# q and k normalised and transposed between the chunks of the last v block

## The reference

```python
def _nat_mixer(h, w_qkv, q_norm, k_norm, rpb, w_o):
    qkv = (h @ w_qkv).reshape(bsz, seq, 3, N_HEADS, HEAD_DIM)     # 1024 -> 3 * 1024
    q = _rmsnorm(qkv[:, :, 0], q_norm)                            # per head of 64
    k = _rmsnorm(qkv[:, :, 1], k_norm)
    v = qkv[:, :, 2]
    ...
    s = jnp.einsum('bhjqrc,...', q_blk, k_band) * scale + bias    # 16 heads, bands of 32 columns
    prob = jax.nn.softmax(...)
    o = jnp.einsum('bhjqrc,brjchd->bjqhd', prob, v_band)
    return out @ w_o
```

## Time and profile before

| | |
|---|---|
| median of three runs | 825.47 us (824.51 to 826.08) |
| the profiled execution | 826.0 us, span 824.2 us |
| PE busy | 746.4 us, 91% of the span |
| DVE, ACT, POOL busy | 375.5, 234.1, 186.5 us |
| DMA | 243.95 MB, mean 296 GB/s |

### The profile page before, as it was taken

How to read it: one execution, slowest core, us unless ns; L and a number is a source line. 1 busy time by engine, 2 the same in 40 slices (tenths; PEclk the granted TensorE clock), 3 DMA queues, 4 the chain that set the end, 5 groups by cost and what they waited for, 6 DMA issues and landing times.

```text
span 824.2 us, 10762 instructions
## 1 busy us (share of the span) xinstructions
PE 746.4 (91%) x4121; PEld 413.8 (50%) x4121; DVE 375.5 (46%) x668; ACT 234.1 (28%) x424; POOL 186.5 (23%) x206
## 2 busy tenths in 40 slices
PE   2977879899999998899999967998999999989997
PEld 2746735633443433345878856466343443433465
DVE  6999452632322222226667858134422233222264
ACT  5551113511101111015575537143001101110163
POOL 7776210320110101000457260030210111100000
PEclk9997979999999999999999979998999999999999
DMA  7062071999999999998589570770999999999851
GB/s 206 27 138 103 9 305 34 424 408 416 422 421 421 420 422 421 419 415 315 195 219 298 189 283 1 306 295 12 330 423 423 419 421 421 421 421 416 332 219 51
DMA packets 66452, 243.95 MB, mean 296 GB/s; under 512 B 21441, under 2 KB 22481, under 8 KB 44641
## 3 DMA queue, kind: packets, MB, share of 16 engines
q1 hardware_dynamic: 62208, 239.71, 73.8%
q0 software_dynamic: 1408, 3.24, 1.8%
q10 hardware_dynamic: 2784, 0.30, 0.3%
HBM read 240.55 MB, written 1.64 MB: 294 GB/s over the span
## 4 chain that ended last, share of the span: by engine, by line
PE 66%; DVE 11%; DMA 7%; SPq 7%; POOL 4%; issue 3%; ACT 3%; ACTq 0%; DVEq 0%
PE PS L1837 21%; PE PS L1581 11%; PE PS L1867 10%; DMA ring<-in_moe_w_up 7%; PE PS L1877 5%; PE PS L2057 3%; PE PS L1765 3%; SPq L472 3%; SPq L473 2%; PE PS L1707 2%; PE PS L1806 2%; SPq L490 2%; PE PS L1961 2%; PE PS L1722 1%; POOL qrs L729 1%
## 5 line engine op out<-in xcount | busy, mean ns | idle before, releaser
L1837 PE MATMUL PS<-ring,xe 128*64 128x512 f32 x1024 | 226.2, 593 | 13.6 <-DMA ring<-in_moe_w_up 11.3
L1837 PEld LDWEIGHTS PS<-ring,xe 128*64 128x64 f32 x1024 | 77.2, 137 | 157.6 <-issue 157.5
L1867 PE MATMUL PS<-ring,actT 128*64 128x512 f32 x512 | 116.9, 598 | 1.7 <-DVE actT L1345 1.4
L644 POOL COPY xe<-xg 128x512 f32 x60 | 47.7, 794 | 296.8 <-PE PS L1837 265.0
L1359 DVE TENSOR_TENSOR olo<-PS,ohi 128x512 fp32r<-128x512 f32 x64 | 44.3, 692 | 123.1 <-ACT ohi L912 123.1
L1345 DVE COPY actT<-PS 128x256 f32<-128x256 f32 x32 | 13.6, 425 | 167.3 <-PE PS L1848 167.3
L912 ACT ACTIVATE ohi<-PS 128x512 fp32r<-128x512 f32 x64 | 38.3, 598 | 152.9 <-PE PS L1867 152.9
L1066 DVE SCALAR_TENSOR_TENSOR ringr<-ring,gT,dwh 128x512 fp32r<-128x512 f32 x80 | 63.1, 841 | 26.4 <-ACT dwh L775 25.1
L904 ACT ACTIVATE act<-PS 128x256 f32<-128x256 f32 x32 | 12.3, 384 | 218.1 <-PE PS L1837 218.1
L1867 PEld LDWEIGHTS PS<-ring,actT 128*64 128x64 f32 x512 | 34.7, 136 | 67.0 <-issue 67.0
L1581 PE MATMUL PS<-ringr,rawh 128*128 128x512 f32 x160 | 63.3, 396 | 0.8 <-DVE ringr L1066 0.8
(11 more groups left out here) (320 smaller groups left out, 978.0 us busy)
## 6 DMA issues: line engine op xcount, KB each, us to landing
ring<-in_moe_w_down SPq DMA_DIRECT2D x64, 1024.0 KB, 20.1
ring<-in_moe_w_gate SPq DMA_DIRECT2D x52, 1024.0 KB
ring<-in_moe_w_up SPq DMA_DIRECT2D x52, 1024.0 KB
ring<-in_moe_w_gate SPq DMA_DIRECT2D x24, 512.0 KB
ring<-in_moe_w_up SPq DMA_DIRECT2D x24, 512.0 KB
ring<-in_nat_w_qkv SPq DMA_DIRECT2D x6, 2048.0 KB
ring<-in_ple_w_gate SPq DMA_DIRECT2D x4, 2048.0 KB
ring<-in_s_w_out SPq DMA_DIRECT2D x2, 2048.0 KB
```

The lines of the kernel that those rows point to most:

```text
L644: pool.tensor_copy(xe[:, e % 4, :, :], xg[:, :, bass.ds(first, CAP)]).then_inc(S("xe_ready"), 1)
L1837: ins = mm(PS[CAP * h_:CAP * h_ + CAP, 0, :].rearrange("p (u f) -> p u f", u=2), xe[:, (2 * p + h_) % 4, k, :], wv[h_][:, k], start=k == 0 ...
L1867: ins = mm(PS[CAP * h_:CAP * h_ + CAP, 2 + n, :], actT[:, k, CAP * h_:CAP * h_ + CAP], wd[h_][:, k, 512 * n:512 * n + 512], start=k == 0, ...
```

## The change

Squares, sums and the power of q and k are done while block 5 (the second of v) is split and multiplied, and PE transposes tile 0 between chunks 1 and 2 of it and tile 1 between chunks 2 and 3. `sq` holds both tiles. Blocks 4 and 5 are evicted later on DVE (block 4 behind the multiplies), block 5 behind `qT` and `kT` on both engines. `qT` and `kT` move from slot 4's memory to the last 8 KB of ring slots 1 and 2, `vb` to the last 8 KB of slot 0. POOL copies v in two parts of 512 columns, four DMAs each, after block 4 and after block 5; `values(0)` waits for the first part, `values(4)` for the second. SP fills slot 4 once the transposes and block 5 are done; the down part of slot 0 waits until the value products are done.

```diff
         qk = at("qk", [P, TT, 2 * NH, HD], F32, A_HI)
         vt = at("vt", [P, TT, D], F32, A_HI + 16384)
-        sq = at("sq", [P, 2 * NH, HD], F32, A_XG)
+        sq = at("sq", [P, TT, 2 * NH, HD], F32, A_XG)
         qss = at("qss", [P, TT, 2 * NH], F32, A_W)
         qms = at("qms", [P, TT, 2 * NH], F32, A_W + 256)
         qrs = at("qrs", [P, TT, 2 * NH], F32, A_W + 512)
         qkw = at("qkw", [P, 2], F32, A_W + 1024)
-        qT = at("qT", [P, NH // 2, T], F32, A_XG + 16384)
-        kT = at("kT", [P, NH // 2, T], F32, A_XG + 24576)
+        qT = at("qT", [P, NH // 2, T], F32, A_R + 1 * RS * 4 + 16384)
+        kT = at("kT", [P, NH // 2, T], F32, A_R + 2 * RS * 4 + 16384)
         oT = at("oT", [P, NH // 2, T], F32, A_O)
         bias = at("bias", [P, NPR, NB_, P], F32, A_H)
         maskb = at("maskb", [P, NB_, BC, ROWS], F32, A_S)
-        vb = at("vb", [P, 2, D], F32, A_HI + 24576)
+        vb = at("vb", [P, 2, D], F32, A_R + 16384)
         V_OF = ((vt, 0), (vb, 0), (vb, 1), (vt, 1))
         prob = at("prob", [P, 4, NB_, P], F32, A_XG)
         probT = at("probT", [P, 2, NB_, P], F32, A_XG + 8192)
...
                         if i == 0:
                             sp.wait_ge(S("x_ready"), 1)
                         else:
-                            sp.wait_ge(S("pv_done"), NPR)
+                            sp.wait_ge(S("k_T"), 2 * TT)
+                            sp.wait_ge(S("split_done"), 4 * dense.index(IT["qkv"][5]) + 4)
+                    if i == 1 and items[m0 + e][0] == 5:
+                        sp.wait_ge(S("pv_done"), NPR)
+                        load_down(m0 + 1, True)
                     load_gate_up(m0 + e)
-                    load_down(m0 + e, True)
+                    if i == 0 or e != 1:
+                        load_down(m0 + e, True)
                 for p in range(3, NP + 1):
                     if p < NP:
                         load_pair(m0 + 2 * p)
...
                 pool.tensor_tensor(qrs[:, t, :], qms[:, t, :], mhalf[:, :], ALU.pow)\
                     .then_inc(S("qrs_ready"), 1)
-            pool.wait_ge(S("qkv_a"), 6)
-            pool.wait_ge(S("qkv_d"), 6)
-            for n, (p0, p1, t, src0) in enumerate(((0, 96, 0, 32), (96, P, 1, 0), (0, 32, 0, 96), (32, P, 1, 0))):
-                pool.dma_start(vb[p0:p1, n // 2, :], vt[src0:src0 + p1 - p0, t, :]).then_inc(S("v_moved"), 16)
+            for c in range(2):
+                pool.wait_ge(S("qkv_a"), 5 + c)
+                pool.wait_ge(S("qkv_d"), 5 + c)
+                cs = slice(512 * c, 512 * c + 512)
+                for n, (p0, p1, t, src0) in enumerate(((0, 96, 0, 32), (96, P, 1, 0), (0, 32, 0, 96), (32, P, 1, 0))):
+                    pool.dma_start(vb[p0:p1, n // 2, cs], vt[src0:src0 + p1 - p0, t, cs]).then_inc(S("v_moved_later" if c else "v_moved"), 16)
             moe(1)
             norm_pow(5)
...
                     ac.dma_start(qkw[64 * d:64 * d + 64, c:c + 1], I[nm][0].rearrange("(p a) -> p a", a=1))\
                         .then_inc(S("qkw_loaded"), 16)
             load_router(ac, 1)
-            for w in range(7):
-                if 0 < w < 6:
-                    dense_hi(IT["qkv"][w], 0, 4)
-                if w:
-                    v_ = w - 1
-                    ac.wait_ge(S("split_done"), 4 * dense.index(IT["qkv"][v_]) + 4)
-                    dst = qk[:, 0, 8 * v_:8 * v_ + 8, :].rearrange("p a d -> p (a d)") if v_ < 4 else \
-                        vt[:, 0, 512 * (v_ - 4):512 * (v_ - 4) + 512]
-                    ac.wait_ge(S("rstd_ready"), NI[3] + 1)
-                    ac.activation(dst, PS[:, 2 * (v_ % 2), :], ACT.Copy, scale=rstd[:, 0:1]).then_inc(S("qkv_a"), 1)
-                if w == 5:
-
+            def qkv_evict(v_):
+                ac.wait_ge(S("split_done"), 4 * dense.index(IT["qkv"][v_]) + 4)
+                dst = qk[:, 0, 8 * v_:8 * v_ + 8, :].rearrange("p a d -> p (a d)") if v_ < 4 else \
+                    vt[:, 0, 512 * (v_ - 4):512 * (v_ - 4) + 512]
+                ac.wait_ge(S("rstd_ready"), NI[3] + 1)
+                ac.activation(dst, PS[:, 2 * (v_ % 2), :], ACT.Copy, scale=rstd[:, 0:1]).then_inc(S("qkv_a"), 1)
+            for w in range(1, 6):
+                dense_hi(IT["qkv"][w], 0, 4)
+                qkv_evict(w - 1)
+                if w == 4:
+
+                    ac.wait_ge(S("qkv_d"), 4)
+                    ac.wait_ge(S("qkv_a"), 4)
                     for t in range(TT):
-                        ac.wait_ge(S("qkv_d"), 4)
-                        ac.wait_ge(S("qkv_a"), 4)
-                        if t:
-                            ac.wait_ge(S("qss_ready"), t)
-                        ac.activation(sq[:, :, :], qk[:, t], ACT.Square).then_inc(S("sq_ready"), 1)
+                        ac.activation(sq[:, t], qk[:, t], ACT.Square).then_inc(S("sq_ready"), 1)
             ac.wait_ge(S("qkw_loaded"), 64)
             link(ac.activation(qkw8[:, :], qkw[:, 0:1], ACT.Copy, scale=1 / math.sqrt(HD)))
...
                     ac.activation(qT[:, 4 * n:4 * n + 4, P * t:P * t + P],
                                   PS[:, 4 + n, :].rearrange("p (a t) -> p a t", a=4), ACT.Copy,
                                   scale=qkw8[:, 0:1]).then_inc(S("qT_ready"), 1)
+            qkv_evict(5)
             for a in range(NPR + 2):
                 if a < NPR:
...
                 ve.wait_ge(S("rstd_ready"), NI[3] + 1)
                 ts(dst, PS[:, n % 4, :], rstd[:, 1:2], None, ALU.mult).then_inc(S("qkv_d"), 1)
-            for w in range(6):
-                if w:
-                    dense_lo(IT["qkv"][w], 0, 4)
-                if w:
-                    qkv_evict(w - 1)
+            for w in range(1, 5):
+                dense_lo(IT["qkv"][w], 0, 4)
+                qkv_evict(w - 1)
             for t in range(TT):
                 ve.wait_ge(S("sq_ready"), t + 1)
-                ve.tensor_reduce(qss[:, t, :], sq[:, :, :], AX.X, ALU.add).then_inc(S("qss_ready"), 1)
+                ve.tensor_reduce(qss[:, t, :], sq[:, t], AX.X, ALU.add).then_inc(S("qss_ready"), 1)
                 ve.wait_ge(S("qss_ready"), t + 1)
                 ts(qms[:, t, :], qss[:, t, :], 1.0 / HD, EPS, ALU.mult, ALU.add).then_inc(S("qms_ready"), 1)
-            qkv_evict(5)
+            dense_lo(IT["qkv"][5], 0, 4)
             for t in range(TT):
                 ve.wait_ge(S("qrs_ready"), t + 1)
                 tt(qk[:, t], qk[:, t], bc(qrs[:, t, :], 2, HD), ALU.mult).then_inc(S("qkn_ready"), 1)
+            qkv_evict(4)
             ve.wait_ge(S("qkw_loaded"), 64)
             for t in range(TT):
                 for n in range(2):
                     ve.wait_ge(S("k_T"), 2 * t + n + 1)
                     ts(kT[:, 4 * n:4 * n + 4, P * t:P * t + P], PS[:, 6 + n, :].rearrange("p (a t) -> p a t", a=4),
                        qkw[:, 1:2], None, ALU.mult).then_inc(S("kT_ready"), 1)
+            qkv_evict(5)
             def scores(a):
                 b = a % 4
...
             dense_mm(IT["qkv"][0], 0, 0, 1)
             raw_T(1, 1)
             dense_mm(IT["qkv"][0], 0, 1, 4)
-            for w in range(1, 6):
-                if w >= 2:
-                    pe.wait_ge(S("qkv_a"), w - 1)
-                    pe.wait_ge(S("qkv_d"), w - 1)
-                dense_mm(IT["qkv"][w], 2 * (w % 2), 0, 4)
-            for t in range(TT):
+            def qk_T(t):
+
                 pe.wait_ge(S("qkn_ready"), t + 1)
                 for b, what in ((4, "q_T"), (6, "k_T")):
                     for n in range(2):
...
                             ins = pe.transpose(PS[:, b + n, P * a:P * a + P],
                                                qk[:, t, hd:hd + 2, :].rearrange("p a d -> p (a d)"), ident[:, :])
                         ins.then_inc(S(what), 1)
+
+            for w in range(1, 6):
+                if w >= 2:
+                    pe.wait_ge(S("qkv_a"), w - 1)
+                    pe.wait_ge(S("qkv_d"), w - 1)
+                if w < 5:
+                    dense_mm(IT["qkv"][w], 2 * (w % 2), 0, 4)
+            dense_mm(IT["qkv"][5], 2, 0, 2)
+            qk_T(0)
+            dense_mm(IT["qkv"][5], 2, 2, 3)
+            qk_T(1)
+            dense_mm(IT["qkv"][5], 2, 3, 4)
             pe.wait_ge(S("qT_ready"), 4)
             pe.wait_ge(S("kT_ready"), 4)
-            pe.wait_ge(S("qkv_a"), 6)
-            pe.wait_ge(S("qkv_d"), 6)
+            pe.wait_ge(S("qkv_a"), 5)
+            pe.wait_ge(S("qkv_d"), 5)
             def scores(a):
...
             def prob_T(a):
                 pe.wait_ge(S("prob_ready"), a + 1)
+                if a == 0:
+                    pe.wait_ge(S("qkv_a"), 6)
+                    pe.wait_ge(S("qkv_d"), 6)
                 if a >= 2:
                     pe.wait_ge(S("probT_ready"), a - 1)
                 for j in range(NB_):
...
             def values(a):
-                if a == 0:
-                    pe.wait_ge(S("v_moved"), 64)
+                if a % 4 == 0:
+                    pe.wait_ge(S("v_moved_later" if a else "v_moved"), 64)
```

## The result

The changed kernel took 821.88 us as the median of six runs (817.8 to 825.58), the kernel before 825.91 beside it: a ratio of 0.9934, 95% interval 0.991 to 0.9958. Measured again, beside the kernel before once more, it took 819.06 beside 827.64, ratio 0.9894 (0.9867 to 0.992). The kernel got faster, by 0.7% in one measurement and 1.1% in the other. The forecast, 817.6 on 825.47, is a ratio of 0.9905: between the two and inside the second interval only. The first median lies 0.6 us above the upper end of the range; carried over to the 825.47 that the range was made for, its ratio gives 820.0.

The account below looks back on a forecast made before the run. Bound: a compute chain up to pair 0, then a DMA-bound tail that shifts with it. Order of the stretch -7.0 and faster first scores -0.85 gave 825.47 - 7.85 = 817.6 us; range 815.2 to 821.3 (0.85).

Parts of the forecast that it names:

- The bound and the one-to-one shift: Compute chain up to pair 0: each microsecond saved in attention moves the DMA-bound tail equally, about 7.9 us; not-reaching-the-end rival 0.04.
- the 7.9 that I had named: First refill after pair 0 and everything behind it: predicted to come about 7.9 us earlier.
- The stretch: Block 4's end to the first scores: 17.15 us instead of 24.17, so -7.0.
- the first stall: TensorE idle before block 5's first chunk, waiting for VectorE's low part: 1.85 us; rival that both stalls vanish, 0.05.
- The second stall: TensorE idle before the first transposes, waiting for the first multiply: 0.9 us.
- The 0.85: First scores at full clock: VectorE uses them 1.2 us after their start instead of 2.08, saving 0.85 more.
- The rule against the row: VectorE's low parts under POOL's power: no slowing assumed; rival by the skill's contention rule, with clock loss, 828.3 us, chance 0.04.
- The clock: Rival: TensorE's clock falls to 0.50 in the new stalls, losing 3.0 us, 0.9 of it possibly hidden; chance 0.13.
- the 24.17 of attention: First use of a score to the product with w_o: the eight pairs were to follow one another as before.
- The v copies: Second part wanted by the fifth value product: in time at 495, cost 0; rival late, up to +2.2 us, chance 0.04.
- The bound, all of SP's 5 MB in front: Second v copies waiting for all 5 MB, 12.5 us, plus 6.4: landing at 507.8, 2.2 us late.
- The range: Measured time of the whole changed kernel: 815.2 to 821.3 us, given 0.85.

Follow-up runs that it names:

- moves_only: The kernel before with only the moves in memory, slot 4's earlier prefill and the v copies in two parts, old order kept; ratio to before 0.9996.
- before_again: The kernel before, unaltered, traced a second time; one execution, no ratio; 25.35 us from block 4's end to VectorE's first use of a score.
- late_prefill: The changed kernel with slot 4 filled only after the last value product, as before; ratio to the kernel before 0.992.

## Why the prediction was right, point by point

*The bound and the one-to-one shift*: right, although the 6.77 is not the 7.9 that I had named, by what layer 0 and the stage behind attention did in these two traces. The first refill and the end moved alike (6.77 and 6.8), and moves_only shows that an earlier prefill alone is worth nothing.

*The stretch*: forecast 17.2 from block 4's end to the scores, measured 17.14; the first stall 1.85 against 1.87; 16 transposes 1.75 against 1.72. The second stall was 0.40 and not 0.9, since chunks 0 and 1 ended later than I had put them and the multiply came 0.3 sooner, each counted from block 4's end. Forecast to the first use 7.85 less, measured 7.95. The 0.85 in it for faster first scores was read from one trace and is partly luck: in before_again those scores were at full clock already, and the gain to the first use is 7.1 to 7.2 against it.

*The rule against the row*: right to follow the row. The low parts under the power take 0.67 each. The rule of the Trainium skill, GPSIMD Engine Reference, Key points, holds for the bias adds and says nothing of how much GpSimd must read before it matters; the power's 32 elements a partition slowed nothing here.

*The clock*: the rival was real and cheap, one trace of six at 1.2 us, where I had reckoned 2.1 to 3.0. What I left out is what the scores at full clock lead to: a wait of 2.45 us in place of 1.21, behind which the clock fell in five of eight traces and took 0.2 to 1.8 back. I had carried the 24.17 of attention over as it was. That it came out to the hundredth in the changed kernel's first trace is luck, for the two traces got there differently: slow scores and a short wait before, full clock and a long wait after.

*The v copies*: the step was right in outcome and its size was off. I took 5.6 us to landing for the second part, from a row in which the 3 MB in front had been issued six microseconds before and were nearly through; it measured up to 10.0, so to 501.1, and what hid it is that the fifth value product comes only at 507.92. The bound, all of SP's 5 MB in front, came to 18.9 after issue (12.5 + 6.4) and was further off still: the truth lies between, since the last of SP's 5 MB landed six microseconds after the copies. With the copies whole, which are 1 MB in place of half, it was 14.5. The Trainium skill, DMA: Bandwidth & Descriptors, Queues, rings and completion order, has two statements on this: a DMA engine takes turns between its queues packet by packet, and a completion is a strongly ordered write that lands only after every earlier write of that DMA engine, whichever its queue. The copies passing part of a queue agree with the first; no run here can show what the second adds.

*The range*: too narrow at the top for one measurement of six runs. The stretch is worth 7.2 to 8.0 by the traces, where the first measurement's ratio is worth 5.4 of 825.47 and the second's 8.7. That the difference is the clock elsewhere is likely but not shown: from the product with w_o to the first refill it took 57.87 us at a clock of 0.94 before, 56.67 at 0.97 in the changed kernel and 55.07 at 1.00 when it was measured again, and in front of the stage, with the same code, block 4's end moves by up to 5.8 us between traces.

## What to carry to other kernels

A serial chain of small steps between two products is best started ahead of the part of the first that doesn't feed it (here v's block): it hides the chain, and it takes away the waits behind which the clock fell. Where exactly its last steps stand between the chunks matters little (7.5 against 0.5 us here). When a change moves a load forward in one queue, look at the small transfers issued behind it on another, and price them between two bounds, their time on idle engines and their time with all of the load in front; here they came out between the two every time, and the same reorder with the copies in one part was slower than the kernel before. And after removing a wait, follow the next bound: here POOL's power, then VectorE's order, then TensorE's clock.

## What the runs showed of the hardware that was not expected

SBUF-to-SBUF copies of 512 columns (four, half a megabyte) landed 2.1 to 2.5 us after issue on idle DMA engines, 7.4 to 8.1 behind 2 MB (late_prefill) and 7.4 to 10.2 behind 5 MB (six traces). The first of these, in the changed kernel:

```profile
DMA to landing us min/median/max: 2.1/2.3/2.5
```

Copies of 1024 columns took 5.4 to 6.4 in the kernel before, 8.7 to 10.6 behind 2 MB and 9.8 to 14.5 behind 5 MB, and still landed 3.7 us ahead of the last of these 5. The granted clock can fall after a wait of 1.9 us that follows unbroken matmuls, and mostly doesn't: the same code kept 1.00 in five traces and was at 0.50 in one. Behind the wait of 2.45 us in attention it fell in nine of twelve traces, at a cost of 0.2 to 1.8 us where nothing else held TensorE up.
